# Rows of three more expert visits by one-hot products instead of gathers

## What is computed

```
scores = sigmoid(t @ w_router)                 # 264 x 64
comb   = weights of the 8 chosen experts of each token, 0 elsewhere
h      = silu(t @ w_gate[e]) * (t @ w_up[e])   # for each expert e, 256 wide
routed = sum over e of (h * comb[:, e]) @ w_down[e]
shared = (silu(t @ ws_gate) * (t @ ws_up)) @ ws_down
x      = layer_norm(ALPHA * x1 + routed + shared)
```

## Time and profile before

| | |
|---|---|
| median of 3 runs | 818.92 us (818.61 to 819.44) |
| profiled execution, its own time | 818.52 us |
| span of the profiled execution | 816.8 us, mean granted TensorE clock 0.995 |
| PE busy | 797.0 us, 98% |
| weight loads on PE | 516.3 us, 63% |
| DVE, ACT, POOL busy | 450.3, 154.4 and 85.3 us |
| moved by DMA | 258.30 MB, mean 316 GB/s |

### The profile page before, as it was taken

The page is one execution under the profiler, slowest core; times in us unless marked ns, Lnnn a source line. Parts: engine busy times, 40 slices in busy tenths (PEclk is TensorE's granted clock), DMA queues, the critical chain, the costliest instruction groups (busy, mean ns, idle before and its releaser), DMA issues.

```text
span 816.8 us, 12603 instructions
## 1 busy us (share of the span) xinstructions
PE 797.0 (98%) x4629; PEld 516.3 (63%) x4629; DVE 450.3 (55%) x1139; ACT 154.4 (19%) x259; POOL 85.3 (10%) x117
## 2 busy tenths in 40 slices
PE   9999999999999999999999999999999998998995
PEld 7876788888788888644444545456664664663443
DVE  6989899999841257754444444432342332332356
ACT  2210111111221004412121212211111111111226
POOL 1019800000010003100000000000000000000021
PEclk9999999999999999999999999999999999999998
DMA  8443344445489965599999999999999999999981
GB/s 332 156 129 104 109 150 154 146 143 129 130 318 420 415 212 201 185 369 419 419 425 425 423 419 427 421 424 428 422 426 426 422 428 423 423 426 419 417 332 54
DMA packets 42972, 258.30 MB, mean 316 GB/s; under 512 B 8746, under 2 KB 9514, under 8 KB 24096
## 3 DMA queue, kind: packets, MB, share of 16 engines
q1 hardware_dynamic: 40464, 252.91, 77.8%
q0 software_dynamic: 2448, 4.58, 1.6%
HBM read 259.27 MB, written 2.53 MB: 321 GB/s over the span
## 4 chain that ended last, share of the span: by engine, by line
PE 85%; DMA 12%; DVE 1%; issue 0%; ACT 0%; SPq 0%; ACTq 0%; DVEq 0%
PE banks L1448 35%; PE banks L1700 21%; PE banks L1760 10%; DMA high<-w_gu 8%; PE banks L1658 5%; DMA ring<-w_gu 4%; PE banks L1599 2%; PE banks L1632 2%; PE banks L1549 2%; PE banks L1463 1%; PE banks L1475 1%; PE banks L1663 1%; PE banks L1725 1%; PE banks L1603 1%; DMA ring<-w_front 1%
## 5 line engine op out<-in xcount | busy, mean ns | idle before, releaser
L1700 PE MATMUL banks<-high,low 128*64 128x512 f32 (+1 forms) x848 | 201.7, 599 | 5.2 <-DMA high<-w_gu 5.2
L1448 PE MATMUL banks<-xT,ring 128*128 128x264 f32 x768 | 176.2, 389 | 0.3 <-DMA ring<-w_front 0.3
L1448 PEld LDWEIGHTS banks<-xT,ring 128*128 128x128 f32 x768 | 144.4, 190 | 30.5 <-issue 5.5
L1700 PEld LDWEIGHTS banks<-high,low 128*64 128x64 f32 (+1 forms) x848 | 63.4, 131 | 132.0 <-issue 122.1
L1345 DVE TENSOR_TENSOR cgb<-cgb,banks 128x264 f32<-128x264 f32 x216 | 78.4, 422 | 117.4 <-PE banks L1658 117.3
L1296 DVE SCALAR_TENSOR_TENSOR y_pair<-banks,sml,y_pair 128x1024 fp32r<-128x1024 f32 x27 | 34.7, 1284 | 102.7 <-ACT y_pair L815 102.7
L1700 PE MATMUL banks<-ring,low 128*64 128x512 f32 (+1 forms) x176 | 79.5, 603 | 2.2 <-DMA ring<-w_gu 2.2
L1760 PE MATMUL banks<-high,mu 128*64 128x512 f32 (+1 forms) x336 | 73.5, 598 | 0.0
L1658 PEld LDWEIGHTS banks<-sw,y_pair 128*128 128x128 f32 x432 | 55.2, 188 | 22.1 <-issue 21.2
L1658 PE MATMUL banks<-sw,y_pair 128*128 128x264 f32 x432 | 62.8, 294 | 0.2 <-DVE cgb L1345 0.2
L815 ACT ACTIVATE y_pair<-banks,sml 128x1024 fp32r<-128x1024 f32 x27 | 30.1, 1114 | 74.4 <-PE banks L1760 74.4
(11 more groups left out here) (351 smaller groups left out, 926.5 us busy)
## 6 DMA issues: line engine op xcount, KB each, us to landing
high<-w_gu SPq DMA_DIRECT2D x37, 2048.0 KB, 21.5
high<-w_dn SPq DMA_DIRECT2D x40, 1024.0 KB, 19.3
ring<-w_front SPq DMA_DIRECT2D x78, 512.0 KB, 3.5
high<-w_gu SPq DMA_DIRECT2D x30, 1024.0 KB, 10.6
ring<-w_gu SPq DMA_DIRECT2D x7, 2048.0 KB, 24.5
bgb<-w_dn SPq DMA_DIRECT2D x11, 1024.0 KB, 19.2
us<-w_dn SPq DMA_DIRECT2D x11, 1024.0 KB, 21.3
ring<-w_gu SPq DMA_DIRECT2D x8, 1024.0 KB, 11.3
```

Source lines behind the costliest of these rows:

```text
L1448: ins = pe.matmul(psum[:, 6 + n % 2, 0:T], ring[:, n % RING, k], rhs[:, k], start=(k == 0), stop=(k == KC - 1))
L1700: ins = pe.matmul(psum[size * j:size * j + size, GU_BANK, :], xg[:, k, size * j:size * j + size], gu[s][:, k], start=(k == 0), stop=(k == ...
```

## The change

`BY_PRODUCTS` grows from 11 to 12, so that the rows behind `a` = 11, the last visit of four experts, come by products. A new constant `EARLY_PRODUCTS` = 2 does the same for the last two of the first six written out visits: the rows made in visits 5 and 6 (steps 6 and 7) come by products. `EARLY_GATHERS` is 5. GpSimd gathers steps 1 to 5 and widens for 6 and 7; VectorE waits for `widened` where it will overwrite the selections of these steps; TensorE waits for the sample rows before visit 5 instead of before the 14 mixed visits, and counts one gather less on each of the two semaphores from there on.

```diff
-        BY_PRODUCTS = 11
+        BY_PRODUCTS = 12
+        EARLY_PRODUCTS = 2
...
             PER_TURN = 6
+            EARLY_GATHERS = 1 + PER_TURN - EARLY_PRODUCTS
...
                 gather(0)
-                for step in range(1, 2 + PER_TURN):
+                for step in range(1, 1 + EARLY_GATHERS):
                     gather_next(step, step % 2)
-                pool.sem_inc(widened, 1 + PER_TURN)
+                pool.sem_inc(widened, EARLY_GATHERS)
+                for step in range(1 + EARLY_GATHERS, 2 + PER_TURN):
+                    widen(step, step % 2)
...
                 for it in range(1, 1 + PER_TURN):
-                    visit(it, it % 2, KC * (it - 1), ahead=(2 * it + 4, 2))
+                    visit(it, it % 2, KC * (it - 1), ahead=(2 * it + 4, 2), wide=it if it > EARLY_GATHERS else None)
                 mixed = n_plain(dve)
                 with dve.Fori(1, mixed) as q:
                     for k in range(1, 1 + PER_TURN):
-                        visit(..., ahead=((q * PER_TURN + (k + 2)) % PAIRS * 2, 2))
+                        visit(..., ahead=((q * PER_TURN + (k + 2)) % PAIRS * 2, 2), wide=q * PER_TURN + k if k < EARLY_PRODUCTS else None)
...
                 for k in range(1, 1 + PER_TURN):
-                    visit(k, ..., gathers=16 * ((k + 1) // 2 + 1))
+                    if k == EARLY_GATHERS:
+                        pe.wait_ge(rows_stored, 16 * (TC + 2))
+                    visit(k, ..., gathers=16 * ((k + 1) // 2 + 1) if k < EARLY_GATHERS else None, wide=k + 1 if k >= EARLY_GATHERS else None)
                 mixed = n_plain(pe)
                 with pe.Fori(1, mixed) as q:
                     for k in range(1, 1 + PER_TURN):
-                        visit(..., gathers=q * 48 + 16 * ((k + 1) // 2 + 1))
-                pe.wait_ge(rows_stored, 16 * (TC + 2))
+                        visit(..., gathers=q * 48 + 16 * ((k + 1) // 2))
...
-                          ... gathers=mixed * 48 + 16 * ((a - BY_PRODUCTS) // 2 + 2) if a >= BY_PRODUCTS else None,
+                          ... gathers=mixed * 48 + 16 * ((a - BY_PRODUCTS) // 2 + 1) if a >= BY_PRODUCTS else None,
```

More of the change, by code:

```diff
@@ L1411, in _ @@
                     for k in range(1, 1 + PER_TURN):
-                        visit(q * PER_TURN + k, k % 2, q * (PER_TURN * KC) + KC * (k - 1), ahead=((q * PER_TURN + (k + 2)) % PAIRS * 2, 2))
+                        visit(q * PER_TURN + k, k % 2, q * (PER_TURN * KC) + KC * (k - 1), ahead=((q * PER_TURN + (k + 2)) % PAIRS * 2, 2), wide=q * PER_TURN + k if k < EARLY_PRODUCTS else None)
                 for a in range(len(mixed_pairs)):
@@ L1790, in _ @@
                 for k in range(1, 1 + PER_TURN):
-                    visit(k, k % 2, [k], [loads_of(k)], halves=1 + k // 3, before=KC * (k - 1), ahead=(2 * k + 4, 2), gathers=16 * ((k + 1) // 2 + 1))
+                    if k == EARLY_GATHERS:
+                        pe.wait_ge(rows_stored, 16 * (TC + 2))
+                    visit(k, k % 2, [k], [loads_of(k)], halves=1 + k // 3, before=KC * (k - 1), ahead=(2 * k + 4, 2),
+                          gathers=16 * ((k + 1) // 2 + 1) if k < EARLY_GATHERS else None, wide=k + 1 if k >= EARLY_GATHERS else None)
                 mixed = n_plain(pe)
@@ L1795, in _ @@
                         visit(q * PER_TURN + k, k % 2, [k], [q * 32 + 16 * (k // 3 + 1)], before=q * (PER_TURN * KC) + KC * (k - 1),
-                              ahead=((q * PER_TURN + (k + 2)) % PAIRS * 2, 2), gathers=q * 48 + 16 * ((k + 1) // 2 + 1))
-                pe.wait_ge(rows_stored, 16 * (TC + 2))
+                              ahead=((q * PER_TURN + (k + 2)) % PAIRS * 2, 2), gathers=q * 48 + 16 * ((k + 1) // 2))
                 def mixed_place(a):
@@ L1805, in _ @@
                     visit(mixed * PER_TURN + (a + 1), (a + 1) % 2, pairs, loaded, before=mixed * (PER_TURN * KC) + KC * a, ahead=mixed_place(a + 2),
-                          halves={PAIRS - 3: 3, PAIRS - 2: 4}.get(pairs[0]), gathers=mixed * 48 + 16 * ((a - BY_PRODUCTS) // 2 + 2) if a >= BY_PRODUCTS else None,
+                          halves={PAIRS - 3: 3, PAIRS - 2: 4}.get(pairs[0]), gathers=mixed * 48 + 16 * ((a - BY_PRODUCTS) // 2 + 1) if a >= BY_PRODUCTS else None,
                           wide=mixed * PER_TURN + (a + 2) if a < BY_PRODUCTS else None, shared=SHARED_AT.get(a, ()))
```

## The result

The changed kernel takes 822.48 us in the median of 10 runs, the kernel before 819.24 us in runs beside it: the ratio is 1.0043, with a 95% interval of 1.003 to 1.0055, so about 3.5 us slower. In a second comparison it was 1.0037 (1.0024 to 1.0049). The profiled execution of the changed kernel has a span of 823.0 us and took 825.03 us, 2.55 us above the median of its kernel, so its rows show where the time goes and not the exact sum. A product of float32 stands as two records in these rows and a transpose as one: 8 transposes show as x8, and the 16 and 8 products of a step as x32 and x16.

What follows compares the result with a forecast made beforehand. PE and the expert weight stream run nearly level, and after the change PE alone sets the pace. Added work 11.66 less waits 7.40 and slow clock 1.44 gives +2.82 us: 821.7 us, range 820.4 to 823.8.

Steps and rivals of the forecast that it cites:

- the likeliest case: Whole kernel: PE alone sets the pace from 343 us to the end, +2.82 us, 821.7 us; chance 0.68.
- PE's added work: Visits 5 and 6 and the step behind the last visit of four: 2 x 3.94 + 3.78 = 11.66 us more.
- the lower bound: Downward bound: shortest product rows (-0.66 us) and visit 5's 0.28 us over the next kind gone, giving +1.9 us.
- the rival of partly hidden products: Product steps on PE may cost 3 us each, so +0.2 us in sum, 819.1 us; chance 0.12.
- The third step lands on the end: Rows behind the last visit of four: after 743.70 us nothing absorbs their products, so 3.78 us land on the end.
- So all three waits go, 7.40 us, and with the last one the slow stretch, 1.44 us: PE's weight waits at the second, third and last visits of four vanish, as does the slow clock after the last.
- the stream never runs dry, but it is close: Weight requests around visits 6 and 7: after PE's delays, 4.5 and 1.6 us of transfer work still stand ahead.
- the rival of late requests: Stream runs dry around visits 6 and 7, the wait at 743.70 partly returns: 823.7 to 825.2 us; chance 0.14.
- the early part: Steps 6 and 7 by products: 2 x 3.94 us of PE work less 7.40 of waits and 1.44 of slow clock, -0.96 us.
- The gathers' transfer time: Transfer engines: each gather takes 0.77 us, so weights at the last wait could land up to 2.3 us sooner.
- The rival that weights set the end: Expert stage: transfers bind every visit, hiding PE's added work; 816.6 us, down to 815.2; chance 0.06.
- The signs that were named beforehand: Changed profile: 18.0 us visits, no waits at visits of four, clock 1.00, 14 gathers; wrong if waits or slow stretches remain.

Runs made afterwards that it cites:

- late_one: Kernel before with only the rows behind the last visit of four experts made by products: 1.0041 of the kernel before, 822.73 us.
- later_two: Kernel before with only the rows made in visits 11 and 12 (steps 12 and 13) by products: 0.999 of the kernel before, 818.74 us.
- pe_delay: Kernel before, all gathers kept, with 17 idle products on PE ahead of the transposes in visits 5 and 6: 1.0021 of the kernel before, 820.31 us.
- early_two: Changed kernel with only steps 6 and 7 by products, the rows behind the last visit of four gathered: 1.0005 of the kernel before, 819.8 us.
- after_again: Changed kernel, unaltered, measured again for a second trace: 1.0037 of the kernel before.
- later_reorder: Kernel before with steps 12 and 13 by products and, in three visits of four, both gate and up requests before down requests: 0.9969, 817.16 us.
- before_reorder: Kernel before with no further products; in three visits of four, both pairs' gate and up requests precede down requests: 0.9995, 819.52 us.
- warm: Kernel before with 13 idle products on PE ahead of the weight wait at the last visit of four: 0.9987 of the kernel before, 818.18 us.
- early_reorder: Changed kernel with only steps 6 and 7 by products; in three visits of four, gate and up requests precede down requests: 0.9983, 818.9 us.

## Why the prediction was right, and where a step failed

The time lies in the range and the likeliest case's sign and size held (+2.82 forecast, about +3.5 measured). The terms:

*PE's added work: right.* 3.94 us a step were forecast for visits 5 and 6; 18.07 and 18.06 us were measured, 7.65 us more for both, since visit 5's old wait of 0.28 us went, as the lower bound allowed. For the third step 3.78 us were forecast and 3.95 measured. Nothing of it was hidden: the rival of partly hidden products falls.

*The third step lands on the end: right.* late_one cost 1.0041, about 3.4 us. This is nearly all of the loss.

*"So all three waits go, 7.40 us, and with the last one the slow stretch, 1.44 us": this step failed.* Two went; at the last one 2.76 us stayed, and in both traces so did the slow stretch. PE was to come to it at 744.18, behind weights that land at 743.70 or sooner; it came at 742.95 (745.71 - 2.76), and the weights at 745.71. The sentence behind it, "the stream never runs dry, but it is close", was wrong at both ends: at 458 to 462 us the cover I had put at 1.6 us wasn't there, and at 590 to 596 us I had not looked. There SyncE's own order keeps a request behind a wait for PE, so that a later PE delays the weights of the visit after next. That is the rival of late requests (chance 0.14); it shows in both traces of the changed kernel, and the new order of requests, which makes the second dry place vanish, gives 1.1 to 1.6 us of the changed kernel back. What made the first dry place stays open: it needs a delay in these visits (later_two, which delays PE six visits later, has none), but with the gathers kept the share stays at 1.01 (pe_delay).

*The size of the waits was off too, the other way.* I took the idle times of the earlier trace rows. PE's timeline of the kernel before shows more, here from the second, the third and the last visit of four:

```profile
620.57 1.06 PE L1700 MATMUL banks<-high,low 128*32 128x512 f32 x6
...
679.94 1.06 PE L1700 MATMUL banks<-high,low 128*32 128x512 f32 x6
683.24 0.62 PE L1700 MATMUL banks<-ring,low 128*32 128x512 f32 x1 [2.24 <-DMA ring<-w_gu]
...
739.12 0.62 PE L1700 MATMUL banks<-high,low 128*32 128x512 f32 x1
```

Six records, of the experts whose weights had landed, ran from 679.94 on and then all waited for the rest. The 58 behind the wait take 7.05 us, and all 64 of a visit without a wait take 7.00 (the row at 628.77): the early six saved nothing. So this wait cost 683.24 - 679.94 = 3.30 us, not 2.24; in the same way the first cost 623.27 - 620.57 = 2.70 and the last 743.70 - 739.12 = 4.58 us. The three were worth 10.58 us, not 7.40. In the changed kernel the first gave back its 2.70 us and the second all but some 0.3 (7.34 against 7.00 us: PE began at 685.40, and the last of these weights, asked for at 657.02, landed 28.7 us later, at about 685.7), together 5.70; the last gave back 4.58 - (745.71 - 741.89) = 0.76, and the slow stretch nothing (8.74 against 8.49 us).

With these terms the trace adds up: 7.65 + 3.95 - 5.70 - 0.76 + 0.25 = 5.39 us, 0.47 for a wait for a gather at 489.03, and 0.41 because the experts began that much later (visit 1 at 358.43 instead of 358.02), 6.27 against the span's 6.2. Smaller differences of either sign are left out. The medians are nearer together, 3.2 to 3.5 us. So the forecast's closeness is partly luck: waits worth 3.18 us more than reckoned made up in part for a last wait and a slow stretch that stayed. Alone, the early part was forecast at 2 x 3.94 - 8.84 = -0.96 us and measured at +0.4, and the late part at +3.78 and measured at about +3.4.

*The gathers' transfer time.* 0.77 us each was forecast, and pe_delay against early_two gives some 1.3 us for two; with intervals that overlap and a delay that differs by 0.3 us this is a size, not a proof.

*The rival that weights set the end* falls: PE's work behind 745.71 us counted in full.

*The signs that were named beforehand.* Visits of 18.0 us with products and 14 gathers came as forecast. The visit behind the last one of four began 765.58 - 759.37 = 6.21 us later in the profiled execution, where some 3 us was forecast, and the clock of 1.00 through 800 us did not hold. Two signs of being wrong came: the wait left at the last visit of four and a wait for a gather in front of the rows (0.47 us).

*The profiled executions are not the median ones.* The changed kernel's profiled execution is 2.55 us above its median, while that of the kernel before is 0.7 us below. The clocks of the runs give a reason. Of the 16 runs of the changed kernel (10, and 6 of after_again), five, both profiled ones among them, have a mean granted clock of 0.994 or 0.995 and took 823.33 to 825.03 us; eleven have 0.997 or 0.998 and took 821.47 to 823.21. The mean times lie 1.65 us apart (824.01 and 822.36), about the price of one slow stretch, 8.74 - 7.05 = 1.69 us. So the slow stretch that stayed in both traces seems to be absent from most executions, and that part of the forecast may have come true in the median. In the kernel before, 54 of the 83 runs beside the experiments have 0.994 or less, under the 0.995 of the profiled one. What the clock gives back in the median is shown by no trace and stays open, and so does why the last wait ends 0.94 us apart in the two traces of the changed kernel (745.71 and 744.77).

## What to carry to other kernels

Work added to an engine that waits is free only up to the wait's cost, only ahead of the last wait, and only while the requests that hang on that engine's progress still come early enough: check the cover of every request behind the added work, the order of the requests on the issuing queue above all. Measure a wait from where the engine would have started its next useful work, not from the idle time: instructions that start early on a part of the operands count as busy and may save nothing. When two streams are nearly level, moving work to where the backlog is deep and asking for what is free before waiting for what isn't gave together the lowest time of all kernels here (later_reorder, 0.9969). And look at the clock of all runs before a profiled execution is taken for the median one.

## What was not expected of the hardware

The granted clock fell to the 1.2 GHz level for a stretch after some waits of PE and not after others of the same length. It fell after 3.92 us in pe_delay, 3.52 in the kernel before, 3.17 in early_two, 2.83 in late_one, 2.76 and 2.78 in the two traces of the changed kernel, 2.23 at 684.18 in before_reorder and 1.98 at 683.24 in warm; it stayed at 2.4 GHz after 2.24 us in the kernel before, 2.53 in early_reorder, 2.27 in later_two and 2.13 in late_one. So the length of the wait alone does not decide it in this range. Each fall cost 1.4 to 1.8 us (8.49 to 8.75 against 7.00 to 7.05).
